# Every fourth weighted v row of the prompt block is added by VectorE instead of TensorE

## What is computed

```python
def one_chunk(args):
    xc, ic, gc = args
    a = jnp.einsum('td,tkd->tk', xc, u[ic])
    return jnp.einsum('tk,tkd->td', gc * jax.nn.gelu(a, approximate=False), v[ic])
```

## Time and profile before

| what | us |
| --- | --- |
| median of 3 runs | 2770.77 |
| lowest and highest | 2766.0 and 2777.85 |
| the profiled execution | 2775.02 |
| its span | 2773.2 |
| PE busy | 2286.2 (82%) |
| DVE busy | 1555.4 (56%) |
| POOL busy | 1683.8 (61%) |
| data moved | 954.02 MB, mean 344 GB/s |

### The profile page before, as it was taken

The page is one execution under the profiler, slowest core; times in us unless marked ns, Lnnn a source line. Parts: engine busy times, 40 slices in busy tenths (PEclk is TensorE's granted clock), DMA queues, the critical chain, the costliest instruction groups (busy, mean ns, idle before and its releaser), DMA issues.

```text
span 2773.2 us, 24064 instructions
## 1 busy us (share of the span) xinstructions
PE 2286.2 (82%) x7331; PEld 1163.9 (42%) x7331; DVE 1555.4 (56%) x3936; ACT 654.2 (24%) x1647; POOL 1683.8 (61%) x1584
## 2 busy tenths in 40 slices
PE   5984899997789999787877799999778787667776
PEld 2463565563344444244333366556433343222222
DVE  0015656666555787543555565576656788554444
ACT  0132324423121121121512232451312211111111
POOL 3003566665566567767776655566657777777775
PEclk8977999998999999999999999999989999999999
DMA  8835899999899999999999989899979999999997
GB/s 272 258 117 200 323 376 335 333 331 345 333 356 374 372 396 394 385 356 399 387 393 376 360 333 383 304 326 327 324 288 380 369 358 349 352 365 406 407 407 311
DMA packets 359635, 954.02 MB, mean 344 GB/s; under 512 B 29248, under 2 KB 159572, under 8 KB 359380
## 3 DMA queue, kind: packets, MB, share of 16 engines
q0 software_dynamic: 222976, 810.02, 77.4%
q1 hardware_dynamic: 99348, 98.60, 10.7%
q10 hardware_dynamic: 37184, 43.86, 4.6%
HBM read 950.00 MB, written 2.36 MB: 343 GB/s over the span
## 4 chain that ended last, share of the span: by engine, by line
PE 42%; DMA 22%; POOL 16%; DVE 10%; issue 8%; ACT 2%; ACTq 0%; SPq 0%; DVEq 0%; POOLq 0%
PE ps L1302 20%; DMA v_rows<-in_peer_v_dram,idx 10%; DMA u_rows<-in_peer_u_dram,idx 10%; POOL v_rows L430 9%; POOL u_rows L423 8%; PE ps L1062 5%; PE ps L1079 5%; DVE u_rows L982 4%; PE ps L1128 3%; PE ps L1257 3%; DMA ring<-in_w_ada_dram 1%; PE ps L1123 1%; PE ps L1203 1%; PE ps L1229 1%; ACT diag L707 1%
## 5 line engine op out<-in xcount | busy, mean ns | idle before, releaser
L1302 PE MATMUL ps<-v_rows,diag 128*128 128x512 f32 x3072 | 1506.2, 625 | 376.0 <-DMA v_rows<-in_peer_v_dram,idx 191.4
L982 DVE CUSTOM_DVE_ANT_0 u_rows<-u_rows,h 128x1024 f32<-128x1024 f32 x768 | 941.3, 1227 | 913.9 <-DMA u_rows<-in_peer_u_dram,idx 906.6
L430 POOL DMA_INDIRECT v_rows<-in_peer_v_dram,idx x768 | 828.1, 1078 | 556.6 <-PE ps L1302 383.4
L423 POOL DMA_INDIRECT u_rows<-in_peer_u_dram,idx x768 | 832.7, 1084 | 514.0 <-DVE idx L778 274.9
L1302 PEld LDWEIGHTS ps<-v_rows,diag 128*128 128x128 f32 x3072 | 564.6, 197 | 1145.6 <-issue 860.0
L707 ACT ACTIVATE diag<-ident,weight 128x128 f32<-128x128 f32 x768 | 245.3, 390 | 510.6 <-DVE weight L990 507.3
L701 ACT ACTIVATE gelu<-dots 128x4 f32<-128x4 f32 x192 | 39.4, 205 | 897.5 <-DVE dots L982 892.1
L1062 PE MATMUL ps<-ring,silu_c 128*2 128x256 f32 x768 | 182.0, 392 | 22.1 <-DMA ring<-in_w_ada_dram 21.7
L1079 PE MATMUL ps<-hT,q_tile 128*128 128x128 f32 (+1 forms) x1024 | 182.4, 333 | 0.0
L1079 PEld LDWEIGHTS ps<-hT,q_tile 128*128 128x128 f32 x1024 | 162.5, 196 | 36.2 <-issue 23.5
L1062 PEld LDWEIGHTS ps<-ring,silu_c 128*2 128x2 f32 x768 | 63.1, 87 | 137.4 <-issue 39.2
(11 more groups left out here) (174 smaller groups left out, 1429.1 us busy)
## 6 DMA issues: line engine op xcount, KB each, us to landing
ring<-in_w_ada_dram SPq DMA_DIRECT2D x48, 1024.0 KB, 12.1
q_tile<-in_peer_wq_dram ACTq DMA_DIRECT2D x32, 1024.0 KB, 12.0
ring<-in_w_in_dram SPq DMA_DIRECT2D x28, 1024.0 KB, 14.3
ring<-in_w_out_dram SPq DMA_DIRECT2D x16, 1024.0 KB, 12.9
u_rows<-in_peer_u_dram,idx POOLq DMA_INDIRECT x768, 6.6
v_rows<-in_peer_v_dram,idx POOLq DMA_INDIRECT x768, 6.6
ln_g<-in_ln_g_dram ACTq DMA_DIRECT2D x6, 512.0 KB, 7.5
ln_b<-in_ln_b_dram ACTq DMA_DIRECT2D x6, 512.0 KB, 10.2
```

The costliest lines, as they stand in the source:

```text
L423: nc.gpsimd.indirect_dma_start(u_rows[:, n % SLOTS, :], None, table_u, bass.IndirectOffsetOnAxis(idx[:, turn % NB, k:k + 1], 0)).then_inc( ...
L430: nc.gpsimd.indirect_dma_start(v_rows[:, n % SLOTS, :], None, table_v, bass.IndirectOffsetOnAxis(idx[:, turn % NB, k:k + 1], 0)).then_inc( ...
L982: V.tensor_tensor_reduce(out=u_rows[:, n % SLOTS, :], in0=u_rows[:, n % SLOTS, :], in1=h2[:, turn % NB, :], scale=1.0, scalar=0.0, op0=ALU ...
L1302: ins_ = M.matmul(ps_y[:, half * 512:(half + 1) * 512], diag[:, n % DIAGS, :], v_rows[:, n % SLOTS, half * 512:(half + 1) * 512], start=(n ...
```

## The change

With SHARE = 4, the picks with n mod 4 = 3 in the two prompt turns are added by DVE: `y_dve` is a [128, 1024] tensor in SBUF, started with a multiplication of v row and weight at pick 3 of a turn and continued with one instruction (v row times weight plus `y_dve`) at every fourth pick. PE and ACT skip these picks. A new semaphore `v_added` frees their v slots; all waits on `v_free` and `diag_ready` count only PE's picks. DVE does its add at position t, behind the dot of pick t+6. At the end of a prompt turn DVE adds `ps_y` to `y_dve` and then multiplies by the gate, one instruction more. To make room in SBUF, `qT` has one buffer instead of two, `cand2` is dropped (the replacement works in place in `cand`), and `nk_out` lies in `rot`.

```diff
+def by_dve(n):
+
+    return n // PICKS % NB == 0 and n % SHARE == SHARE - 1
...
-        nk_out = sb("nk_out", [P, 2 * P])
+        nk_out = rot[:].rearrange("p h d -> p (h d)")[:, 0:2 * P]
-        qT = sb("qT", [P, 2, 4 * P])
+        qT = sb("qT", [P, 4 * P])
-        cand2 = sb("cand2", [P, TOPK * TOPK])
+        y_dve = sb("y_dve", [P, D])
...
             def gather_v(n):
                 turn, k = n // PICKS, n % PICKS
-                if n >= SLOTS:
-                    pool.wait_ge(v_free, n - SLOTS + 1)
+                if n >= SLOTS and by_dve(n - SLOTS):
+                    pool.wait_ge(v_added, dve_adds(n - SLOTS + 1))
+                elif n >= SLOTS:
+                    pool.wait_ge(v_free, pe_adds(n - SLOTS + 1))
...
+                    if by_dve(n):
+                        continue
                     if n >= DIAGS:
-                        act.wait_ge(v_free, n - DIAGS + 1)
+                        act.wait_ge(v_free, pe_adds(n - DIAGS + 1))
...
-                step(V.match_replace(cand2[:], top[:, 0:8], cand[:], LOW))
+                step(V.match_replace(cand[:], top[:, 0:8], cand[:], LOW))
...
-                dve.wait_ge(v_free, at_)
-                st.step(V.tensor_tensor(product, ps_y, gate[:, stream(b), :], ALU.mult), y_free)
+                dve.wait_ge(v_free, pe_adds(at_))
+                if b == 0:
+                    st.step(V.tensor_tensor(y_dve[:], ps_y, y_dve[:], ALU.add), y_free)
+                    step(V.tensor_tensor(product, y_dve[:], gate[:, stream(b), :], ALU.mult))
+                else:
+                    st.step(V.tensor_tensor(product, ps_y, gate[:, stream(b), :], ALU.mult), y_free)
...
+            def add(n):
+
+                dve.wait_ge(v_landed[n % SLOTS], 16 * (n // SLOTS + 1))
+                w = weight[:, n // GROUP % 2, n % GROUP:n % GROUP + 1]
+                if n % PICKS == SHARE - 1:
+                    ins_ = V.tensor_scalar(y_dve[:], v_rows[:, n % SLOTS, :], w, None, ALU.mult)
+                else:
+                    ins_ = V.scalar_tensor_tensor(y_dve[:], v_rows[:, n % SLOTS, :], w, y_dve[:], ALU.mult, ALU.add)
+                st.step(ins_, v_added)
...
+                if t >= 0 and by_dve(t):
+                    add(t)
                 beside.until(t)
...
             for t in range(TOTAL):
-                add(t)
+                if not by_dve(t):
+                    add(t)
                 beside.until(t)
```

More of the change, by code:

```diff
@@ L36 @@
 ADA_T, IN_T, OUT_T, Q_T = 24, 7, 4, 8
+SHARE = 4
 SMALLS = 35
@@ L86, with dve_adds, pe_adds @@
 PLANS = [Plan(s) for s in range(len(STAGES))]
+def by_dve(n):
+    return n // PICKS % NB == 0 and n % SHARE == SHARE - 1
+def dve_adds(n):
+    return sum(by_dve(i) for i in range(n))
+def pe_adds(n):
+    return n - dve_adds(n)
 def late_at(s, h):
@@ L336, in program @@
         v_free = sem("v_free")
+        v_added = sem("v_added")
         gelu_ready = sem("gelu_ready")
@@ L521, in query @@
                 st.take(q_ready)
-                st.step(nc.scalar.copy(qT[:, h % 2, 0:2 * w], ps_q[:, 0:2 * w]), qT_ready)
+                st.step(nc.scalar.copy(qT[:, 0:2 * w], ps_q[:, 0:2 * w]), qT_ready)
                 if h + 1 < HEADS:
@@ L583, in mixer @@
                     nc.scalar.copy(k12T[:], ps_turn[:, 512:512 + 2 * P].rearrange("p (c n) -> p c n", c=2))
-                    st.step(nc.scalar.copy(nk_out[:], ps_turn[:, 768:1024]), turn_free)
-                    act.dma_start(outs[4][0, l].rearrange("t h d -> t (h d)"), nk_out[:]).then_inc(k_out_done, 16)
+                    st.step(nc.scalar.copy(nk_out, ps_turn[:, 768:1024]), turn_free)
+                    act.dma_start(outs[4][0, l].rearrange("t h d -> t (h d)"), nk_out).then_inc(k_out_done, 16)
                     act.wait_ge(k_out_ready, l + 1)
@@ L759, in pick @@
                 V.max_index(pos[:, 0:8], top[:, 0:8], cand[:])
-                step(V.match_replace(cand2[:], top[:, 0:8], cand[:], LOW))
+                step(V.match_replace(cand[:], top[:, 0:8], cand[:], LOW))
                 yield
-                step(V.max(top[:, 8:16], cand2[:]))
-                step(V.max_index(pos[:, 8:16], top[:, 8:16], cand2[:]))
+                step(V.max(top[:, 8:16], cand[:]))
+                step(V.max_index(pos[:, 8:16], top[:, 8:16], cand[:]))
                 ins_ = V.tensor_tensor(gw[:, b, h], top[:], top[:, 0:1].to_broadcast([P, TOPK]), ALU.subtract)
@@ L1090, in key_scores @@
                         ins_ = M.matmul(ps_q[:, (2 * i + half) * P:(2 * i + half + 1) * P],
-                                        qT[:, h % 2, half * T_.width + i * P:half * T_.width + (i + 1) * P], k12T[:, half, :],
+                                        qT[:, half * T_.width + i * P:half * T_.width + (i + 1) * P], k12T[:, half, :],
                                         start=True, stop=True)
@@ L1298, in add @@
                     pe.wait_ge(y_free, turn)
-                pe.wait_ge(diag_ready, n + 1)
+                pe.wait_ge(diag_ready, pe_adds(n + 1))
                 pe.wait_ge(v_landed[n % SLOTS], 16 * (n // SLOTS + 1))
```

## The result

The changed kernel takes 2808.95 us (median of 4 runs, 2804.86 to 2817.34) against 2771.43 for the kernel before: ratio 1.0127, 95% interval 1.0103 to 1.0150. It is 37 us slower, where 2750 us and a gain of 0.9% were forecast; the time lies above the stated range (2715 to 2792).

A forecast was written before the change was run, and what follows sets the result against it. PE was taken to set the pace in the prompt turns, through the v slots. First turn -6 - 8 - 4 + 2.8 + 1.4, about -14 us, second -11: together -25 from 2775.0, so 2750 us, range 2715 to 2792.

The forecast's parts named there:

- What bounds the kernel: Prompt turns: PE all but full through projection, attention and output projection; POOL waits 97.5 us for its adds to free slots.
- rival (a): Prompt turns: PE's time comes back in full up to the transfers' ceilings, -53 us, 2722 us; chance 0.15.
- What the change removes: PE adds on the path: 10.7 us in projection, 15.5 in attention, 6.2 in output projection, 32 us a turn.
- The loop: Slot 3 freed through VectorE: 12.4 us for four picks against 13.3 in attention, so 8 us gained there, not 15.5.
- In favour of the change: At add 63, behind the dot of pick 69, VectorE would free the slot 2 us earlier than PE.
- The added work: VectorE, 32 adds of 1.4 us a turn: 2.8 us cost in the norms, 1.4 at turn's beginning and end together.
- Cover: Most of VectorE's 45 us of adds a turn would replace its 151.4 us of waiting for u rows.
- (c): VectorE's slot becomes a slower bound, 15.0 us for four picks in attention: 2805 at worst, 2790 if half; chance 0.14.
- (d): Shared port: 64 VectorE adds each hold up a POOL gather 0.7 us, +45 us on the forecast, 2795; chance 0.06.
- Clock: PE's granted clock left alone: a PE a tenth less full need not lose it.

The follow-up runs named there:

- relief_only: Kernel before, but nobody adds every fourth v row of the prompt turns and its slot is reused once the row has landed: 2752.09 us, 0.9913.
- gate_only: Kernel before, but POOL also waits for the dot of pick t+6 before reusing the slot of every fourth prompt pick t: 2794.15 us, 1.0077.
- work_only: Kernel before, PE adding all rows, plus an unused VectorE instruction of the same size at the changed kernel's places: 2788.44 us, 1.0053.
- work_relief: Kernel before, every fourth prompt row added by nobody, its slot reused once landed, plus unused same-size VectorE instructions: 2765.25 us, 0.9966.
- v5_relief: Kernel before with five v slots and every fourth prompt row added by nobody, its slot reused once landed: 2682.43 us, 0.9651.

## Why the prediction was wrong, point by point

- *What bounds the kernel.* "PE sets the pace, through the slots" held in part. Taking PE's adds away with no cost at all gives 22 us, not the 64 us of PE counted as on the path or the 53 of rival (a). The slots were the other half of that sentence: a fifth slot gives 69 us, of which some 25 in the two prompt turns.
- *What the change removes* (10.7, 15.5, 6.2 us a turn): too large as path. relief_only, by the same picks as in the table of the result, gained 4.4, 6.2 and 4.5 us in the projection, the attention and the output projection of the first prompt turn, and 1.2, -2.8 and 2.4 in the second.
- *The loop.* This is the step that failed: 12.4 us for four picks, set against mean spans of 13.3, 15.7 and 15.4 us. The 12.4 was put together from the shortest issues (3.7 us for three) and the median landing of the attention (6.1), and that is what the fastest pass of the changed kernel took, 12.3. The mean pass took 15.0: 4.6 for the issues and 7.7 to the dot. In the kernel before the same picks took 14.4. So the loop was not 0.9 us or more under the pace, leaving room for a gain, but 0.6 over it. And the stretch from 372 to 436 us, where "I count nothing" was written since its transfers were full, ran in its second half at 10.25 us for four picks. There even the fastest pass is too slow; the picks 34 to 54 lost 6.7 us. The forecast gain of 8 us in the attention did not come either (1 us less in one turn, 3 more in the other).
- *"In favour of the change"*: one instance, the add of pick 63, was taken for the rule that VectorE frees the slot 2 us before PE would. In half of the places of that turn the dot ended later than PE's add, already before the change. In gate_only POOL waits for it in 15 picks.
- *The added work.* Size right (1.28 and 1.22 us rows for 1.22 expected, no wait for v rows). What it costs, about 15 us alone, is more than the 8.4 us of the two terms (2.8 and 1.4, twice); in front of the gate it costs 25 (the table: 46 with the gate against 21).
- *Cover.* "Most of it in place of its 151.4 us of waiting": VectorE waits 155.5 us still. In work_only, where no slot waits for the work, 130.2 of the 151.4 us are left: half of the 45 us of work was covered. In the changed kernel the u rows stand in POOL's queue behind the v row that waits for the work, and the work covers nothing.
- *Rivals.* (c) named the mechanism and the sign, and its full form (2805) is 4 us from the result; I gave it 0.14. Its loop of 15.0 us is the measured mean, and its landing of 7.4 us, taken from one row, is near the measured 7.7. The rest of the nearness is luck: it counted 1.3 us for a divide and a maximum in front of the add, where in every pass the add started 1.15 us behind the start of the dot, with nothing between, and it left out 0.9 us of issues; and it put the whole 15 us a turn in the attention, which lost none in the first prompt turn. (d) did not happen, as the last section shows. The turns without VectorE adds stayed as forecast.
- *Clock.* "Need not lose it" was wrong: 0.95 granted in the first prompt turn before, 0.90 after. A matmul record of a v row took 623 ns on average in that turn before and 675 after, and the adds' busy time fell from 247.4 to 204.9 us, by 42 and not by a fourth, which is 62.

## What to carry to other kernels

When a step is moved to another engine, write down for each buffer that it frees which instruction of the new engine's order the release now stands behind, and compare that distance with the old one. Put the sum of the new loop against like: built from the shortest rows and medians it is a fastest pass, and belongs beside the fastest picks in the trace, since a ring lives on catching up; beside the mean of a stretch belongs a sum of means. Read a wait that speaks for the change at every place where it occurs, not at one. And before memory is spent on a second accumulator to relieve a busy engine, try it as one more slot of the ring in front of it; here that was worth 2.5% against a loss of 1.3%.

## What was not expected of the hardware

The granted clock of PE fell as its idle time grew: 0.95 and 0.96 in the two prompt turns of the kernel before, where PE was busy 87% and 90%, 0.90 in both of the changed one (76% and 79%), 0.92 in work_relief and 0.93 in v5_relief over the first prompt turn, though both are faster. No run here separates how much the lower clock costs.

The port between VectorE and POOL did not add up to anything in POOL's v gathers. Groups of instructions in the first prompt turn, before (busy us, mean ns, then idle time):

```profile
L430 POOL DMA_INDIRECT v_rows<-in_peer_v_dram,idx x132 | 149.6, 1133 | 126.6 <-PE ps L1302 97.5 <-issue 29.2
L423 POOL DMA_INDIRECT u_rows<-in_peer_u_dram,idx x137 | 142.0, 1036 | 282.5 <-DVE idx L778 238.7 <-issue 40.2 <-DVE dots L982 3.5
```

and after:

```profile
L447 POOL DMA_INDIRECT v_rows<-in_peer_v_dram,idx x132 | 148.9, 1128 | 148.3 <-DVE y_dve L1016 101.8 <-issue 33.9 <-PE ps L1337 12.6
L438 POOL DMA_INDIRECT u_rows<-in_peer_u_dram,idx x136 | 148.0, 1088 | 279.4 <-DVE idx L797 236.9 <-issue 40.2 <-DVE dots L1005 2.3
```

The v gathers have the same mean, 1.13 us, and the u gathers 1.09 for 1.04, 7 us over 136 of them.
